# First block of a two-block transformer on one core: values, pool input and gates as seven half-size products, with a shorter weight ring

## What is computed

```python
c_act = silu(c)                                   # c: one row of 1024
mod = c_act @ w_ada + b_ada                       # 6 x 1024 modulation values
shift1, scale1, gate1, shift2, scale2, gate2 = split(mod, 6)
h = rms_norm(x, norm1_g) * (1 + scale1) + shift1
q, k, v, u, z_gate = split(h @ w_in)              # 512, 512, 512, 512, 2048
y_attn = attention(q, k, v, rel_bias) @ w_branch_attn    # 8 heads of 64, causal
y_pool = pool_mixer(u, pool_w, pool_scale) @ w_branch_pool
g_attn, g_pool = split(sigmoid(z_gate + b_gate), 2)
x = x + gate1 * ((g_attn * y_attn + g_pool * y_pool) @ w_out)
h2 = rms_norm(x, norm2_g) * (1 + scale2) + shift2
x = x + gate2 * moe(h2)                           # 32 experts, 2 per token
```

## Time and profile before

| | |
|---|---|
| median of 3 runs | 1369.35 us (1368.8 to 1370.72) |
| profiled execution | 1369.89 us, span 1368.1 us, mean granted TensorE clock 0.992 |
| busy, of the span | TensorE 97%, weight loads 73%, VectorE 45%, ScalarE 22%, GpSimd 1% |
| moved | 365.11 MB, mean 267 GB/s |
| chain of work that ended last | TensorE 88%, DMA 9%, VectorE 2% |

### The profile page before, as it was taken

How to read it: one execution, slowest core, us unless ns; L and a number is a source line. 1 busy time by engine, 2 the same in 40 slices (tenths; PEclk the granted TensorE clock), 3 DMA queues, 4 the chain that set the end, 5 groups by cost and what they waited for, 6 DMA issues and landing times.

```text
span 1368.1 us, 20531 instructions
## 1 busy us (share of the span) xinstructions
PE 1324.9 (97%) x8534; PEld 995.2 (73%) x8534; DVE 614.1 (45%) x1398; ACT 297.8 (22%) x588; POOL 7.8 (1%) x18
## 2 busy tenths in 40 slices
PE   5999999999999999888999999999999999999997
PEld 4888887444334344333588889999998878999996
DVE  6456255111100100100468838674555773877454
ACT  2224202112112112111243621220013362122000
POOL 0000000000000000000000000000000000000000
PEclk8999999999999999999999999999999999999999
DMA  9898785999999999999954144444444414444410
GB/s 388 362 405 318 315 361 192 421 410 422 422 423 421 421 423 421 423 423 420 421 211 150 62 154 164 176 161 179 159 164 148 148 62 154 162 178 158 181 63 32
DMA packets 52238, 365.11 MB, mean 267 GB/s; under 512 B 6176, under 2 KB 6480, under 8 KB 9136
## 3 DMA queue, kind: packets, MB, share of 16 engines
q1 hardware_dynamic: 49392, 355.49, 65.6%
q10 hardware_dynamic: 2032, 5.56, 1.4%
q0 software_dynamic: 720, 2.72, 0.5%
HBM read 359.54 MB, written 2.11 MB: 264 GB/s over the span
## 4 chain that ended last, share of the span: by engine, by line
PE 88%; DMA 9%; DVE 2%; ACT 0%; issue 0%; DVEq 0%; ACTq 0%
PE bank L1150 27%; PE bank L630 20%; PE bank L871 19%; DMA ring<-in_weights 6%; PE bank L642 5%; PE bank L882 3%; PE bank L1295 2%; PE bank L714 2%; PE bank L1086 2%; DMA pool_a<-in_weights 2%; PE bank L856 1%; PE bank L1199 1%; DVE ring L1753 1%; DMA c_row<-in_c 1%; PE bank L1250 1%; PE bank L1276 1%
## 5 line engine op out<-in xcount | busy, mean ns | idle before, releaser
L630 PE MATMUL bank<-h,ring 128*128 128x256 f32 x832 | 183.8, 381 | 0.1
L871 PE MATMUL bank<-ring,cst 128*64 128x512 f32 x608 | 174.7, 594 | 7.6 <-DMA ring<-in_weights 4.2
L630 PEld LDWEIGHTS bank<-h,ring 128*128 128x128 f32 x832 | 156.9, 190 | 22.7 <-issue 1.5
L871 PEld LDWEIGHTS bank<-ring,cst 128*64 128x64 f32 x608 | 54.5, 137 | 97.5 <-issue 96.4
L2048 DVE TENSOR_TENSOR act<-act,bank 128x512 f32<-128x512 f32 (+1 forms) x17 | 11.1, 656 | 240.7 <-PE bank L871 240.7
L1150 PE MATMUL bank<-hid,ring 128*128 128x128 f32 x912 | 115.6, 275 | 0.0
L1150 PE MATMUL bank<-h,ring 128*128 128x128 f32 x896 | 113.8, 275 | 0.0
L1150 PEld LDWEIGHTS bank<-hid,ring 128*128 128x128 f32 x912 | 108.6, 192 | 0.0
L1150 PEld LDWEIGHTS bank<-h,ring 128*128 128x128 f32 x896 | 107.0, 192 | 0.1
L1150 PE MATMUL bank<-sq,ring 128*128 128x128 f32 x720 | 95.1, 275 | 0.0
L871 PE MATMUL bank<-ringx,cst 128*64 128x512 f32 x232 | 86.2, 596 | 2.6 <-DMA ring<-in_weights 2.6
(11 more groups left out here) (384 smaller groups left out, 1794.6 us busy)
## 6 DMA issues: line engine op xcount, KB each, us to landing
ring<-in_weights SPq DMA_DIRECT2D x250, 1024.0 KB, 10.6
ringx<-in_weights SPq DMA_DIRECT2D x45, 1024.0 KB, 22.3
spare<-in_weights SPq DMA_DIRECT2D x18, 1024.0 KB, 19.0
pool_a<-in_weights SPq DMA_DIRECT2D x9, 1024.0 KB, 19.4
x<-in_weights SPq DMA_DIRECT2D x9, 1024.0 KB, 22.8
ring<-in_weights SPq DMA_DIRECT2D x4, 512.0 KB, 23.6
spare<-in_weights SPq DMA_DIRECT2D x4, 512.0 KB, 18.3
x<-in_x SPq DMA_DIRECT2D x1, 1024.0 KB, 5.0
```

Of the source, the lines that this page charges most:

```text
L630: ins = e.matmul(u.ap[:, 0:S], w[:, k * width + j * P:k * width + (j + 1) * P], acts[:, k, :], start=k == 0, stop=k == kc - 1)
L871: ins = e.matmul(g.bank[bank][ex * SLOTS:(ex + 1) * SLOTS, :], stat(m, ex), pair[ex][:, m * 512:(m + 1) * 512], start=first and m == 0, st ...
```

## The change

The values, pool input and gates (12 tiles, i4 to i15) are computed as seven half-size products, with the products' code shared with the second block. For the values and the pool input the tokens remain the stationary operand (`turned`). VectorE makes four differences once, four sums per tile, two tiles ahead, and assembles each tile's result: four instructions, in place of two copies for the values and of nothing for the gates, whose sigmoid ScalarE now takes in place one step later. The sums' two buffers are ring slots 10 and 11 and the differences lie in a spare slot, so the ring of the first block has RF = 10 slots and these three areas take expert tiles only once gate 7 is done. The order of tiles is a list (unchanged in its first 22 places). Where each gate step reduced one modulation tile (a12 to a19), now every second does (a13 to a16) and a12 is reduced in the values' loop, so that seven instead of four fall behind the gates. c comes as one row and is spread over the partitions by a matmul with a row of ones; Silu reads PSUM. Of the first unread matmuls 4 come ahead of it and 6 behind. The normed chunks are made in pairs between the modulation tiles.

```diff
-SPARE_AFTER = {36: 0, 41: 1}
-FIRST_SLOTS = (*SPARE, R + 5, R + 3, R + 2, 0, 1, 2, 3, 4, 5, AHEAD, R, R + 1, 6, 7, 8, 9, 10, R + 4, 11, KEPT)
+RF = 10
+FSEVENS = 12
+SPARE_AFTER = 34
+FIRST_SLOTS = (SPARE[0], RF, RF + 1, SPARE[1], R + 5, R + 3, R + 2, 8, 9, 0, 1, AHEAD, R, R + 1, 2, 3, 4, 5, R + 4, 6, 7, KEPT)
...
-        n = t % R if t < T_EXP else expert_slot(t - T_EXP) if t < T_LAYERS else (t - T_LAYERS) % RL
+        n = t % RF if t < T_EXP else expert_slot(t - T_EXP) if t < T_LAYERS else (t - T_LAYERS) % RL
...
+    g.first_sums = [g.ring[RF + n] for n in range(2)]
+    g.first_diff = [g.ring[SPARE[1]][:, n * 512:(n + 1) * 512].rearrange("p (k t) -> p k t", k=4) for n in range(4)]
+    g.first_a, g.first_pair = g.scr[:, 0:P], g.rs
...
+FIRST_ORDER = ("a4 a0 i0 a5 a1 i1 a6 a2 i2 a7 a3 i3 a8 i4 a9 i5 a10 i6 a11 i7 a12 i8 i9 a13 i10 i11 a14 i12 i13 a15 i14 i15 "
+               "a16 b0 a17 b1 a18 b2 a19 a20 b3 a21 b4 a22 b5 a23 b6 b7").split()
...
+        if SLOT[t] in (RF, RF + 1, SPARE[1]):
+            g.full(sp, "gate", 7, 1)
+            return
...
-    order = list(range(T_EXP))
-    for after, n in SPARE_AFTER.items():
-        order.insert(order.index(after) + 1, T_EXP + FIRST_TILES[n])
-    for t in [*order, *(T_EXP + n for n in FIRST_TILES[len(SPARE):])]:
+    order = [*range(T_EXP), *(T_EXP + n for n in FIRST_TILES[1:])]
+    order.insert(SPARE_AFTER + 1, T_EXP + FIRST_TILES[0])
+    for t in order:
...
 def pe_first(e, g, A):
-    pe_unread(e, g, 10)
+    pe_unread(e, g, 4)
+    for half in range(2):
+        u = g.take(e, ("c", half), 6 + half)
+        if half == 0:
+            e.wait_ge(g.s["c_in"], 16)
+        g.last(u, e.matmul(u.ap, g.c("ones")[0:1, :], g.cact[0:1, half * 512:(half + 1) * 512], start=True, stop=True))
+    pe_unread(e, g, 6)
...
     for j in range(4):
-        w = g.filled(e, in_tile(4 + j))
-        pe_tokens(e, g, ("vu", j), w, g.h, ready)
-        g.owed += 1
+        pe_first_seven(e, g, j)
...
     for j in range(8):
-        w = g.filled(e, in_tile(8 + j))
-        for jj in range(2):
-            pe_chunk(e, g, ("gate", 2 * j + jj), w, jj, 256, KC, g.h, ready)
-        g.owed += 1
+        pe_first_seven(e, g, 4 + j)
         pe_attention_step(e, g, A, j + 1)
...
+def pe_first_seven(e, g, n):
+
+    key = ("vu", n) if n < 4 else ("gate", n - 4)
+    w = g.filled(e, in_tile(4 + n))
+    acts = token_quarters(g.h)
+    acts[0][1] = g.first_diff[0]
+    for half in range(2):
+        g.take(e, (*key, half))
+    e.wait_ge(g.s["diff_ready"], 1)
+    pe_products(e, g, key, w, g.first_sums[n % 2], n, acts, g.first_diff[1:], 0, 1, n < 4)
+
+
+def pe_products(e, g, key, w, sums, m, acts, diffs, b, of, turned=False):
...
     def product(u, at, a, act, first):
         for k in range(4):
-            ins = e.matmul(u.ap[:, at * P:(at + 1) * P], a[:, k, :], act[:, k, :], start=k == 0 and (of == 1 or (b == 0 and first)),
+            stat, moving = (act, a) if turned else (a, act)
+            ins = e.matmul(u.ap[:, at * P:(at + 1) * P], stat[:, k, :], moving[:, k, :], start=k == 0 and (of == 1 or (b == 0 and first)),
                            stop=k == 3 and b == of - 1, skip_group_check=of > 1)
...
     product(x, 0, a11, b11, True)
-    e.wait_ge(g.s["sum_ready"], SEVENS * l + i + 1)
+    e.wait_ge(g.s["sum_ready"], m + 1)
...
 def act_first(e, g, A):
...
+    e.dma_start(g.cact[0:1, :], g.dram["c"]).then_inc(s["c_in"], 16)
     e.dma_start(g.prm[:, 0:first], g.dram["prm"][:, 0:first]).then_inc(s["prm_in"], 16)
-    e.dma_start(g.cact, g.dram["c"].to_broadcast([P, D])).then_inc(s["c_in"], 16)
-    e.wait_ge(s["c_in"], 16)
-    e.activation(g.cact, g.cact, ACT.Silu).then_inc(s["cact_ready"], 1)
+    for half in range(2):
+        g.full(e, "c", 1)
+        ps = g.full(e, "c", half)
+        g.read(("c", half), e.activation(g.cact[:, half * 512:(half + 1) * 512], ps, ACT.Silu))
...
     for j in range(8):
-        for oc in (2 * j, 2 * j + 1):
-            ps = g.full(e, "gate", oc)
-            g.read(("gate", oc), e.activation(g.gate3[:, oc, :], ps[:, 0:S], ACT.Sigmoid, bias=g.p("b_gate", oc, 1)))
+        g.evac(e, *(("gate", j - 1, 0) if j else ("vu", 3, 0)))
+        act_first_product(e, g, ("gate", j), g.first_a)
+        if j:
+            act_gate(e, g, j - 1)
         act_attention_step(e, g, A, j + 1)
+    act_gate(e, g, 7)
...
 def dve_first(e, g, A):
...
     for m in range(4):
+        two = slice(2 * m, 2 * m + 2)
         if m:
+            dve_normed(e, g, m)
             dve_ada(e, g, FRONT[2 * m])
...
         if m == 0:
-            e.wait_ge(s["root"], 1)
-            for k in range(KC):
-                e.tensor_tensor(g.h[:, k, :], g.x[:, k, :], g.rs, ALU.mult).then_inc(s["h_scaled"], 1)
+            dve_normed(e, g, m)
 
     dve_ada(e, g, 8)
+    e.wait_ge(s["h_shifted"], KC)
+    dve_differences(e, g, g.h, g.first_diff[1:], g.first_diff[0])
+    dve_first_sums(e, g, 0)
+    dve_first_sums(e, g, 1)
     dve_angles(e, g)
...
     for j in range(4):
-        if j:
-            dve_ada(e, g, 8 + j)
-        for tt in range(ST):
-            ps = g.full(e, "vu", j, tt)
-            g.read(("vu", j, tt), e.tensor_copy((g.v3 if j < 2 else g.u3)[:, tt, (j % 2) * 256:(j % 2 + 1) * 256], ps[:, 0:256]))
+        dve_ada(e, g, 9 + j)
+        dve_tokens_seven(e, g, j)
+        dve_first_sums(e, g, j + 2)
     dve_scores(e, g, A, 0)
     for j in range(8):
-        dve_ada(e, g, 12 + j)
+        dve_seven(e, g, ("gate", j), 5 + j, g.gate[:, 2 * j * S:(2 * j + 2) * S], g.first_a, g.first_pair)
+        if j < 6:
+            dve_first_sums(e, g, 6 + j)
         if j < 3:
             dve_scores(e, g, A, j + 1)
+        if j % 2 == 1:
+            dve_ada(e, g, 13 + j // 2)
         if j == 4:
             dve_bounds(e, g)
```

More of the change, by code:

```diff
@@ L1385, in act_first @@
     e.activation(e0, e0, ACT.Exp).then_inc(s["lb_exp"], 1)
+    for j in range(1, 4):
+        g.evac(e, "vu", j - 1, 0)
+        act_first_product(e, g, ("vu", j), g.first_a)
     act_attention_step(e, g, A, 0)
@@ L1805, in dve_first @@
     mixed = g.h
-    g.evac(e, "gate", 15)
+    e.wait_ge(s["gated"], 16)
     for oc in range(KC):
@@ L1815, in dve_first @@
     for oc in range(KC):
+        if oc % 4 == 0:
+            dve_ada(e, g, 19 + oc // 4)
         ps = g.full(e, "pool", oc)
@@ L2304, in dve_differences, with dve_tokens_seven, dve_seven @@
     e.tensor_tensor(t4, b21, t2, ALU.subtract).then_inc(g.s["diff_ready"], 1)
-def dve_seven(e, g, key, n, out):
+def dve_tokens_seven(e, g, j):
+    to = (g.v3 if j < 2 else g.u3)[:, :, (j % 2) * 256:(j % 2 + 1) * 256]
+    left, right = to[:, :, 0:P], to[:, :, P:2 * P]
+    two = lambda a: a.rearrange("p (n t) -> p n t", n=2)
+    twice = lambda a: a.unsqueeze(1).to_broadcast([P, 2, P])
+    one, pair, key = g.first_a, g.first_pair, ("vu", j)
+    x = g.full(e, *key, 0)
+    e.wait_ge(g.s["first_product"], j + 1)
+    g.read((*key, 0), e.tensor_tensor(left, twice(one), two(x[:, P:3 * P]), ALU.add))
+    g.evac(e, *key, 0)
+    y = g.full(e, *key, 1)
+    g.step.up(e.tensor_tensor(two(pair), twice(left[:, 1, :]), two(y[:, 0:2 * P]), ALU.add))
+    g.after(e)
+    e.tensor_tensor(left[:, 1, :], pair[:, 0:P], y[:, 2 * P:3 * P], ALU.add)
+    e.tensor_tensor(right[:, 0, :], pair[:, P:2 * P], y[:, 3 * P:4 * P], ALU.add)
+    g.read((*key, 1), e.tensor_tensor(right[:, 1, :], pair[:, P:2 * P], y[:, 0:P], ALU.add))
+def dve_seven(e, g, key, n, out, one=None, pair=None):
+    one, pair = (g.one_a, g.pair_a) if one is None else (one, pair)
     two = lambda a: a.rearrange("p (n t) -> p n t", n=2)
@@ L2312, in dve_seven @@
     e.wait_ge(g.s["first_product"], n)
-    g.read((*key, 0), e.tensor_tensor(two(out[:, 0:256]), twice(g.one_a), two(x[:, P:3 * P]), ALU.add))
+    g.read((*key, 0), e.tensor_tensor(two(out[:, 0:256]), twice(one), two(x[:, P:3 * P]), ALU.add))
     g.evac(e, *key, 0)
     y = g.full(e, *key, 1)
-    g.step.up(e.tensor_tensor(two(g.pair_a), twice(out[:, P:2 * P]), two(y[:, 0:2 * P]), ALU.add))
+    g.step.up(e.tensor_tensor(two(pair), twice(out[:, P:2 * P]), two(y[:, 0:2 * P]), ALU.add))
     g.after(e)
-    g.step.up(e.tensor_tensor(out[:, P:3 * P], g.pair_a, y[:, 2 * P:4 * P], ALU.add))
-    g.read((*key, 1), e.tensor_tensor(out[:, 3 * P:4 * P], g.pair_a[:, P:2 * P], y[:, 0:P], ALU.add))
+    g.step.up(e.tensor_tensor(out[:, P:3 * P], pair, y[:, 2 * P:4 * P], ALU.add))
+    g.read((*key, 1), e.tensor_tensor(out[:, 3 * P:4 * P], pair[:, P:2 * P], y[:, 0:P], ALU.add))
 def dve_layer_score(e, g, l, h):
```

66 lines of the change are left out of this document (40 added, 26 removed).

## The result

The changed kernel takes **1379.65 us** (median; 1378.89 to 1380.48), beside 1370.03 for the kernel before on the same chip: ratio 1.007, 95% interval 1.0058 to 1.0083, so 9.6 us slower. The forecast was 1376.0, slower by 6.4: right in direction and within its range, 3.65 us too low. The profiled execution took 1380.12 us, its span is 1378.3.

What follows compares the result with a forecast made beforehand. TensorE was taken to bound the kernel until the experts, then their weights' DMA. Front -3.7, products -9.6, waits +18.9 and queue +0.8 gave +6.4 us on 1369.4, so 1376 us; range 1367 to 1381.

Steps and rivals of the forecast that it cites:

- front: Before the projections: c as one row and normed chunks in pairs let the row matmul end 3.7 us earlier, at 55.3.
- products: Values, pool and gate tiles as seven half-size products at 6.25 us each: 2.8 + 6.8 = 9.6 us saved.
- waits: TensorE waiting on VectorE, from the differences to the router's bias matmul: eight waits, 18.9 us in all.
- rival 3: TensorE's clock falls in the stall at gate 1, 2.4 us more: +8.8, 1378.2 us; chance 0.12.
- queue: Before the experts: all 48 tiles go out ahead of expert tiles 1 to 21, delaying the first of the 170; 0.8 us added.
- VectorE's chain: VectorE idles until a8 lands at 50.5, makes the bias row by 66.4, and the bias is in place at 96.0.
- The waits for the sums of tiles 2 and 3: Values and pool loop: VectorE needs 6.7 us per tile against TensorE's 6.25, so TensorE waits 2.2 and 0.5 us.
- The stall at gate 1: Between gates 0 and 1 TensorE stands 7.5 us, for score banks, probabilities and gate 0's banks, behind the late bias.
- Gates 2 and 3: Gate 2 takes a bank of the third scores, which VectorE reads late, and gate 3 likewise: waits of 3.1 and 1.9 us.
- Rival 2: a8 comes early, its slot being free, so the first 4.9 us of waits go: +1.5, 1370.9 us; chance 0.16.
- Rivals 1 and 4: 1: all waits hidden but the router's 1.5, 1357.6 us, chance 0.12. 4: front fails, c late, 1378.8 us, chance 0.08.
- The other rule weighed: A drain of about 1.38 us behind each ScalarE table load would make the sum +12; the forecast costed it at nothing.

Runs made afterwards that it cites:

- experiment 1: The changed kernel with another order of the first tiles, so that a8 and i4 take slots that are free early: 1372.65 us, ratio 1.0017.
- experiment 3: The changed kernel with 8 matmuls that nothing reads put in TensorE's stall ahead of gate 1: 1379.32 us, ratio 1.0065.
- experiment 2: The changed kernel with VectorE's angle steps ahead of a8 and the bias row between the first two sets of sums, a8 still late: 1371.86 us, ratio 1.0013.
- experiment 4: The changed kernel with 12 unread matmuls in the first stall before gate 1 and one each ahead of the last score matmul and two turns: 1377.54 us, ratio 1.0048.
- Experiment 6: The changed kernel with three early expert tiles issued behind first-block tile 40 and not behind all 48: 1376.86 us, ratio 1.0047.

## Why the prediction was right, and where it was off

The sum was +6.4. By the trace, with the same steps:

| term | forecast | measured |
|---|---|---|
| front | -3.7 | -3.55 (alone: ratio 0.9975, -3.4) |
| products | -9.6 | -7.8 |
| waits | +18.9 | +11.3 |
| low clock | none (rival 3: +2.4) | +7.1, of which 4.4 ahead of gate 1 |
| queue | +0.8 | +1.9 |
| sum | +6.4 | +9.0, beside +9.6 |

**The front** came out as written by two misses: Silu's halves ended at 8.1 us (8.7 forecast), because the spreads took 1.98 us and not about 3, so the long run started 4.3 us earlier (3.7 forecast), and then it took 29.1 us instead of 28.3.

**The products were mis-sized.** The forecast took 56.8 / 8 = 7.1 us for a gate tile of before, which is busy time with the ends of each group in it, against a pitch from 29 tiles back to back, 6.25. Measured alike (20.92 and 18.97 for three tiles) a tile saves 0.65 and not 0.85. That is 5.2 instead of 6.8 for the gates; the four values tiles saved 2.6 in experiment 1, where they ran without a wait (25.21 us instead of 27.82), 2.8 forecast. Together 7.8.

**VectorE's chain** was right to within 0.5 us as far as the bias: a8 read at 50.43 (50.5), row done at 65.97 (66.4), bias in place at 95.69 (96.0), since VectorE's steps before it are counted from rows and the wait in front is a slot's. It holds as far as gate 1: by the forecast gate 0 ends at 92.5, the step's own work is 1.7 and its waits are 7.5, so gate 1 starts at 101.7; it started at 100.97. The waits for the sums of tiles 2 and 3 (2.7) did not come in this execution: a tile takes VectorE 6.45 us (72.32 to 78.77), not 6.7, and TensorE was itself late, by slow passes. Where the clock stayed high in this stage, as in experiment 3's execution, tile 2 did wait, 1.4 us, as the second of these two waits:

```profile
PE bank L1183 <- DVE ring L2363: 2.7, 2, 1.4
```

The stall at gate 1, 7.5 forecast, lengthened the step from 1.66 to 9.20 us, so by 7.5; but 4.8 of it were waits, and the other 2.7 go with the low clock (0.54 in the window from 96 to 101 us). Gates 2 and 3 waited for 1.7 each and not for 3.1 and 1.9. That a slow gate 1 gave VectorE time is not the reason: in experiment 2, where gate 1 was fast, the two waits are 1.8 each.

**The clock** is the step that failed. The forecast kept the fall as rival 3, with a chance of 0.12, at the stall alone and priced by the long run's 2.4. It happened together with the forecast and in two places. In the values stage the first 24 passes behind the wait took 4.57 us, and later ones of the same shape 2.84: 1.7 lost. At gate 1 the scores, the turn and the tile's first passes were slow: 7.5 - 4.8 = 2.7 before the tile and 9.22 - 6.49 = 2.7 in it. But only the last 2.7 are a cost. Gate 1 starts 5.3 us behind the bias, with the clock at 1.00 in the stall (experiment 4: 5.27) as with the low one (5.28), so slow work ahead of it only takes the place of waits that the forecast had counted. The Trainium skill, TensorE: Matmul & The Clock Gate, Why this matters for your kernels, whose rule would have put this rival first, was right in direction.

**The queue** was named and undersized: 1.9 against 0.8. The forecast had the copy of x in its backlog and let the first of the 170 tiles land between 247 and 250; the copy alone ended at 245.6, and the tile in x's place and then the first of the 170 were issued only behind it. Experiment 6 puts the cost of the backlog, as far as it can be told, at 3 us, part of which the kernel before has too.

The terms sum to 9.0; 0.6 is not assigned. In this list waits too high by 7.6 and a clock left out at 7.1 cancel. For 4.4 us of that it is no luck but the same time under another name, as gate 1's start hangs on the bias, which was forecast well. Behind gate 1 it was luck that the miss stayed small: the products brought 0.2 less in each of seven tiles (1.4), the low clock cost 2.7 and the queue 1.1 more, while the waits ahead of gates 2 and 3 were 1.6 less. With the 0.7 by which gate 1 came sooner and the router's 0.2 that is 2.7 of the 3.2 us missed.

Rival 3's 1378.2 is nearer to the measured time than the forecast. The forecast's cause for the loss, VectorE behind a8 and the bias row behind VectorE, is shown by experiments 1 and 2: each takes back some 7 to 8 us alone.

Rival 2 (a8 early: 1370.9, no change) has nearly the time of the kernel that makes it so, 1372.65 at ratio 1.0017, but not by its sum: it let only the first 4.9 us of waits go and kept the 7.5 at gate 1, where in experiment 1 the row came 7.7 us earlier and the step took 6.0 us instead of 9.2. Rivals 1 and 4 fell: the waits stay, and the front does what it says. The other rule weighed, a drain behind each table load (the Trainium skill, ScalarE: Activation LUTs, What ACT_TABLE_LOAD costs), again has nothing in the trace: the load at 64.97 takes 1.28 us and the sine starts at 66.27.

## What to carry to other kernels

When an edit saves work on the engine that is the bound, first ask what the others must now do ahead of the longest chain of fixed length that hangs on them; here 29 to 32 us of transfers through memory started at one 0.54 us instruction, and moving that one earlier was worth as much as the ring slot that caused the wait. Price idle time on TensorE twice, as the wait and as work at half the clock behind it, but count slow work only where nothing else sets the end of its stretch: gate 1 started 5.3 us behind the bias at either clock. And before counting a gain at the front, look whether the queue behind has a backlog: a gain of 2.4 us at the gather was worth 0.3 at the first tile behind it.
